# Collapsing the modulation rows with a two-column selector matmul in place of four identity transposes and a four-way sum

## The chip, the core and the metric

One core of one Trainium2 chip runs the whole program in one launch. The metric is device time in microseconds (us) of that launch. Shorter is better.

## The reference

Three blocks run one after another on 256 tokens of width 1024: a two-layer trunk with a 256-token context beside the latent sequence, a gated delta-net with its feed-forward, and a dilated attention with its feed-forward. The change touches only the modulation of the trunk, which each of its two layers computes for two conditioning vectors, `c_ctx` (the context's) and `c` (the latent's):

```python
def modulation(cvec, w_mod, b_mod):
    m = (jax.nn.silu(cvec) @ w_mod + b_mod)[..., None, :]
    return jnp.split(m, 6, axis=-1)

sh1, sc1, ga1, sh2, sc2, ga2 = modulation(c, w_mod, b_mod)
sh1c, sc1c, ga1c, sh2c, sc2c, ga2c = modulation(c_ctx[None], w_mod, b_mod)
u = (rmsnorm(x, g_mix) * (1 + sc1) + sh1) @ w_in
```

`w_mod` is 2 x 1024 x 6144, so a vector-matrix product of 1024 x 6144 is made for two vectors in each layer. Its results scale and shift the normed activations, and gate what is added to the residual.

## The kernel before, in words

**Layout.** Activations in column form have the model dimension on the 128 partitions, so a modulation value must end up as a per-partition scalar: MODC (a part of the small-tile buffer SM) holds 192 columns, [layer, sequence, which of six, block of 128 channels]. The 6144 outputs of a layer are made in 12 chunks of 512; with two layers there are 24 chunks, numbered m = 0 to 23.

**One chunk** takes four steps on three engines.

1. `pe_modulate(m)` (TensorE, PE): two weight tiles of 1 MB (RAW, from DMA), eight matmuls of 512 moving columns. The stationary operand is SC2, the two silu vectors padded with zeros to 32 columns. Four of the eight go to partition groups 0, 32, 64 and 96 of one PSUM bank at a time, so the bank holds four partial sums: partition 32 g + s holds group g's part for vector s, and the partitions with s of 2 or more hold zeros.
2. `act_modulate(m)` (ScalarE, ACT): copies the bank, 128 x 512, to ROWS, which is CF[:, 1024:1536]. There is one ROWS buffer, so the copy of chunk m waits for the turn of chunk m - 1 (`pe_mod`).
3. `pe_modturn(m)` (PE, the "turn"): four transposes of 128 x 128, with ROWS as the stationary operand and the identity IDN (CF[:, 0:128]) as the moving one. They fill a bank of 128 x 512. The last one raises `pe_mod`.
4. `dve_modturn(m)` (VectorE, DVE): a TENSOR_REDUCE that picks the columns 32 g + s (s below 2) of each of the four blocks and adds over g: 32 values in and 8 out on each partition. It raises `dve_mod`, frees the bank, and later `dve_modend` adds the bias and makes the gains.

**Order.** Each engine runs its own instruction stream, written out by hand with semaphores; `weave` interleaves generators step by step. `pe_start` does chunks 0 to 3 at the head of the kernel, before anything else can be projected: modulate(0), modulate(1), turn(0), modulate(2), turn(1), modulate(3), turn(2), turn(3), then the transposes of the small vectors ("cols") and of the normed input. Chunks 4 to 23 are woven by `mods(...)` into the projections, the mixers and the MLPs of the trunk, up to about half of the span. On the sequences of PE, ACT and DVE a turn lies between long runs of weight matmuls. Weights are split into two fp32r halves (WHI by ACT, WLO by DVE), and `matmul3` makes three matmuls of them.

**The head of the DVE stream** (`dve_start`): three memsets (the last one clears SC2), then a wait for the transposes of the silu vectors ("crow"), then the copy of these into SC2, which `pe_modulate(0)` needs. The identity arrives by a DMA that SP issues as its third (`ld_id`).

**CF[:, 1024:1920]** holds ROWS (1024:1536) and SC2 (1536:1792) in the trunk; columns 1792 and up are not used then. POOL loads the level masks over all of it once turn 23 is done.

The helper lines under which the trace records instructions: L69 `matmul`, L77 `transpose`, L80 `act`, L83 `copy`, L86 `tt`, L99 `reduce`, L108 `memset`.

Of the kernel before, what the change touches and what calls it, by code (L numbers as in the profile page):

```python
# [9 lines left out]
ALU = mybir.AluOpType  # L10
# [171 lines left out]
def program(nc, T, out):  # L182
    ctx = ExitStack()
    with ctx:
        def sb(name, n, dt=F32):
            return ctx.enter_context(nc.sbuf_tensor(name, [128, n], dt))
# [16 lines left out]
        CF = sb("CF", 2304)  # L203
# [21 lines left out]
        def cf(i, n=128):  # L225
            return CF[:, 128 * i:128 * i + n]
        IDN, TRIF, TRIB, SSUF, SPRE, ONE16, MSKT, MSKN = [cf(i) for i in range(8)]
# [5 lines left out]
        def small(n):  # L233
            a = at[0]
            at[0] += n
            assert at[0] <= 1744
            return SM[:, a:a + n]
# [4 lines left out]
        MODC = small(192).rearrange("p (l s j k) -> p l s j k", l=2, s=2, j=6)  # L242
# [21 lines left out]

        ROWS = CF[:, 1024:1536]
        SC2 = CF[:, 1536:1792].rearrange("p (k s) -> p k s", k=8)
        CROW = AR[0:2, 0:1024]

        signals = []

        def signal(name, by=1):
            s = Signal(ctx.enter_context(nc.semaphore(name)), by)
            signals.append(s)
            return s


        ld_c, ld_id, ld_x, ld_ctx, ld_small, ld_wg, ld_cf, ld_mu, ld_gf, ld_row, ld_di, ld_lm, ld_xr, st_out = [
            signal(n, 16) for n in ("ld_c", "ld_id", "ld_x", "ld_ctx", "ld_small", "ld_wg", "ld_cf", "ld_mu",
                                    "ld_gf", "ld_row", "ld_di", "ld_lm", "ld_xr", "st_out")]
        w_land = [signal(f"w_land{i}", 16) for i in range(NRAW)]  # L280

        act_c, dve_c, pe_c, pool_c = [signal(n) for n in ("act_const", "dve_const", "pe_const", "pool_const")]
# [25 lines left out]
        pe, act, dve, pool, sp = [Engine() for _ in range(5)]  # L308

        def wait_free(key):  # L310

            had = banks.before.get(key)
            if had is None or pe.eng is None:
                return
            for s in signals:
                if ("free", had) in s.at:
                    pe.wait_ge(s, ("free", had))
                    return
            raise KeyError(had)
# [161 lines left out]
        def pe_modulate(m):  # L481
# [4 lines left out]
            for k0 in (0, 4):  # L486
# [3 lines left out]
                for k in range(4):  # L490
                    i = pe.matmul(b[32 * k:32 * k + 32, :], SC2[:, k0 + k, :], v[:, k, :], k0 == 0, k0 == 4)
                i.then_inc(pe_gemm, ("used", t.i), ("mod", m))
# [7 lines left out]
        def pe_modturn(m):  # L500
            b = banks.take(("modt", m), ring)
            wait_free(("modt", m))
            pe.wait_ge(act_mod, ("row", m))
            for i in range(4):
                o = pe.transpose(b[:, 128 * i:128 * i + 128], ROWS[:, 128 * i:128 * i + 128], IDN)
            o.then_inc(pe_mod, ("turn", m))

        def dve_modturn(m):
            l, ch = chunks[m]
            dve.wait_ge(pe_mod, ("turn", m))  # L510
            b = banks.of(("modt", m))
            parted = b.rearrange("p (k g c) -> p c k g", k=4, g=4)[:, 0:2]
            dve.reduce(MODC[:, l, :, ch // 2, 4 * (ch % 2):4 * (ch % 2) + 4], parted, ALU.add).then_inc(
                dve_mod, ("free", ("modt", m)), ("col", m))

        VCv = VC[:, 0:64].rearrange("p (v l k) -> p v l k", v=4, l=2)
# [4 lines left out]
        def dve_modend(l, c0, c1):  # L521
            js = slice(c0 // 2, c1 // 2)
            dve.wait_ge(dve_mod, ("col", 12 * l + c1 - 1))
            dve.wait_ge(dve_c, "cols")
            for sq in range(2):
                dve.tt(MODC[:, l, sq, js], MODC[:, l, sq, js], BMv[:, l, js], ALU.add).then_inc(dve_mod, ("bias", l, c1))
            dve.wait_ge(dve_mod, ("bias", l, c1))
            for j in range(2):
                if c0 <= 6 * j + 2 < c1:
                    for sq in range(2):  # L530
                        dve.stt(GS[:, l, sq, j, :], MODC[:, l, sq, 3 * j + 1, :], 1.0, VCv[:, j, l, :], ALU.add, ALU.mult).then_inc(
                            dve_mod, ("gain", l, j))
# [4 lines left out]
        def pe_mods(ms):  # L537
            for m in ms:
                pe_modulate(m)
                yield  # L540
                pe_modturn(m)
                yield
# [54 lines left out]
        def dve_norm(t, ti, had=None, row=None):  # L597

            dve.wait_ge(pool_tn, ("rstd", t, ti))
            if had is not None:  # L600
                dve.wait_ge(pe_tn, ("turn", t, had, 1))
                if row is None:
                    dve.wait_ge(dve_tn, ("lo", t, had, 1))
            xb, s = XNb[ti % 2], s_tn[ti][:, 0:1]
            if row is None:
                dve.ts(xb, XRt[:, ti, :], s, None, ALU.mult).then_inc(dve_tn, ("xn", t, ti))
            else:
                dve.stt(xb, XRt[:, ti, :], s, row, ALU.mult, ALU.mult).then_inc(dve_tn, ("xn", t, ti))
# [70 lines left out]
        def small_loads():  # L679
            for i, n in enumerate(("g_mix", "g_mlp", "norm_mix_2", "norm_ffn_2")):  # L680
                yield vr[16 * i:16 * i + 16, :], T[n].rearrange("l (k p) -> (l k) p", p=128)
            yield vr[64:68, :], T["s_pool"].rearrange("l (k p) -> (l k) p", p=128)
            yield v_ap[0:96, 1, :], T["b_mod"].rearrange("l (k p) -> (l k) p", p=128)
            yield CWR, T["gdn_conv_w_2"].rearrange("a w (k p) -> (a w k) p", p=128)
            for l in range(2):
                yield GQK[:, l, 0, :], T["g_q"][l, :].partition_broadcast(128)
                yield GQK[:, l, 1, :], T["g_k"][l, :].partition_broadcast(128)
                yield GGLA[:, l, :], T["g_gla"][l, :].partition_broadcast(128)
                yield WP[:, l, :, :], T["w_pool"][l].rearrange("(a b) c d -> (b c) a d", b=2)
            yield GNW, T["gdn_norm_w_2"][0, :].partition_broadcast(128)  # L690
            yield DQK[:, 0, :], T["dil_q_norm_2"][0, :].partition_broadcast(128)
            yield DQK[:, 1, :], T["dil_k_norm_2"][0, :].partition_broadcast(128)
            yield ALD[:, 0:8], T["gdn_a_log_2"][0, :].partition_broadcast(128)
            yield ALD[:, 8:16], T["gdn_dt_bias_2"][0, :].partition_broadcast(128)

        def sp_start():
            sp.dma(CROW[0:1, :], T["c_ctx"].rearrange("(a n) -> a n", a=1)).then_inc(ld_c, "c_ctx")
            sp.dma(CROW[1:2, :], T["c"]).then_inc(ld_c, "c")
            sp.dma(CF[:, 0:128], T["cf"][:, 0:128]).then_inc(ld_id, "idn")

        def pe_start():
# [3 lines left out]
            for k in range(8):  # L705
                m = pe.transpose(b[:, 2 * k:2 * k + 2], CROW[:, 128 * k:128 * k + 128], IDN[0:2, 0:2])
            m.then_inc(pe_c, "crow")
# [15 lines left out]
        def act_start():  # L723
            act.dma(XRt[:, 2:4, :], T["x"][0].rearrange("(t p) d -> p t d", p=128)).then_inc(ld_x, "x")
            act.dma(XRt[:, 0:2, :], T["ctx"][0].rearrange("(t p) d -> p t d", p=128)).then_inc(ld_ctx, "ctx")
            act.wait_ge(ld_c, "c")
            act.act(CROW, CROW, ACT.Silu).then_inc(act_c, "silu")
            for o, i in small_loads():
# [16 lines left out]
        def dve_start():  # L745
            dve.memset(R8[0:33, 512:1536], 0.0).then_inc(dve_c, "wz")
            dve.memset(RT[32:33, :], 1.0).then_inc(dve_c, "ones")
            dve.memset(SC2, 0.0).then_inc(dve_c, "sc0")
            dve.wait_ge(pe_c, "crow")
            dve.wait_ge(dve_c, "sc0")  # L750
            dve.copy(SC2[:, :, 0:2], banks.of("crow")[:, 0:16].rearrange("p (k s) -> p k s", k=8)).then_inc(dve_c, ("free", "crow"), "sc")
            dve_norm("in0", 0)
            dve_norm("in0", 1)
            for m in range(4):
                dve_modturn(m)
            b = banks.of("cols")
            dve.wait_ge(pe_c, "cols")
            dve.copy(VC, b[:, 0:68])
            dve.copy(BMC, b[:, 128:224])
            dve.copy(CWC, b[:, 256:352]).then_inc(dve_c, ("free", "cols"), "cols")  # L760
            dve_modend(0, 0, 4)
            for ti in range(4):
                dve_turned("in0", ti, True)
                if ti < 2:
                    dve_norm("in0", ti + 2, ti)
            dve.wait_ge(ld_mu, "mu")
            dve.copy(MU[:, :], AR[:, 12544:13568]).then_inc(dve_c, "mu")
            dve_splits(proj_tile(NAMES[0], 0, 0, 0))
# [47 lines left out]
        def proj_tile(name, l, sq, c):  # L816
            return tile_of["w_in", (l, sq), 4 * c, COLS[name][0]]
# [2851 lines left out]
```

## Time and profile before

| | |
|---|---|
| median of 3 runs | 2021.7 us |
| lowest and highest run | 2015.37 and 2022.43 us |
| the profiled execution's own time | 2015.37 us |
| its span | 2013.6 us |
| TensorE clock granted, mean of the span | 0.958 of full |
| PE busy | 1839.6 us, 91% |
| DVE busy | 1230.7 us, 61% |
| ACT busy | 927.3 us, 46% |
| DMA | 320.43 MB, mean 159 GB/s |

The profiled execution is the lowest of the three runs shown. Its span leaves 1.8 us of its own time outside. In the rows below, PE is a matmul, PEld a weight load, which overlaps the matmuls. The tile names read "output <- inputs", and for a matmul the moving operand stands first and the stationary one second, then the rows x columns of the stationary tile, then the partitions x moving columns. A matmul's duration covers its whole way through the array; matmuls overlap, so what one costs in a stream is the distance from one start to the next, not its duration.

### The profile page before, as it was taken

To read this page: it belongs to the slowest core of one execution; us is meant where nothing else is said; L and a number is where in the kernel's file an instruction comes from. 1 tells how busy PE (TensorE), PEld (TensorE's weight loads), DVE (VectorE), ACT (ScalarE), POOL (GpSimd) and SP (SyncE) were. 2 spreads that over 40 slices of the span, in tenths; PEclk is the share of its full clock that TensorE was granted. 3 is DMA by queue.
4 is the path that set the end of the run, shared out by engine and by line. 5 is a ranking of instruction groups with operands and counts; after the bars stand their busy time and mean duration, and the time that the engine had idled before them with its cause. 6 is when DMAs were issued, how large, how long until landed. Compare 5 with 4: busy or idle time off the path is not lost.

```text
span 2013.6 us, 26348 instructions
## 1 busy us (share of the span) xinstructions
PE 1839.6 (91%) x10729; PEld 1512.3 (75%) x10729; DVE 1230.7 (61%) x1700; ACT 927.3 (46%) x1433; POOL 381.1 (19%) x428
## 2 busy tenths in 40 slices
PE   4879787999999999877989989898999999989999
PEld 1756566777887777765778879897878878877887
DVE  2555547566676665566465756863577646567774
ACT  3544344355456443544354547445344434454442
POOL 2121122211141122121111222121211005321110
PEclk9889998899999999898889999999999999999999
DMA  8454553355556576531355654221255554414554
GB/s 288 143 198 143 188 179 119 123 187 169 195 168 225 189 246 215 174 99 43 117 186 192 190 176 133 85 75 52 86 172 186 187 180 167 167 53 153 192 189 136
DMA packets 218244, 320.43 MB, mean 159 GB/s; under 512 B 8582, under 2 KB 123978, under 8 KB 217740
## 3 DMA queue, kind: packets, MB, share of 16 engines
q1 hardware_dynamic: 212916, 308.97, 47.3%
q0 software_dynamic: 1744, 6.03, 0.9%
q10 hardware_dynamic: 3464, 3.75, 0.6%
q8 instruction: 85, 1.39, 0.3%
q14 instruction: 35, 0.29, 0.0%
HBM read 317.68 MB, written 1.05 MB: 158 GB/s over the span
## 4 chain that ended last, share of the span: by engine, by line
PE 74%; DVE 10%; ACT 7%; DMA 5%; issue 3%; POOL 2%; SPq 0%; ACTq 0%; DVEq 0%; POOLq 0%
PE ps L69 71%; PE ps L77 3%; DVE WLO L86 3%; DMA RAW<-in_w_mod_dram 2%; ACT WHI L80 2%; DMA RAW<-in_w_up_dram 1%; DMA RAW<-in_w_in_dram 1%; ACT AR L80 1%; DVE AR L86 1%; DVE TT L86 1%; ACT PMD L80 1%; ACT L80 1%; POOL SM L86 1%; DVE PMD L86 1%; ACT TT L80 1%
## 5 line engine op out<-in xcount | busy, mean ns | idle before, releaser
L86 DVE TENSOR_TENSOR WLO<-RAW,WHI 128x1024 fp32r<-128x1024 f32 (+2 forms) x498 | 604.3, 1255 | 320.0 <-ACT WHI L80 319.6
L80 ACT ACTIVATE WHI<-RAW 128x1024 fp32r<-128x1024 f32 (+2 forms) x498 | 482.0, 1017 | 403.3 <-PE ps L69 309.1
L69 PE MATMUL ps<-TT,WHI 128*128 128x512 f32 (+1 forms) x1808 | 578.5, 380 | 10.2 <-DVE TT L86 7.1
L69 PE MATMUL ps<-TT,WLO 128*128 128x256 f32 x1632 | 429.7, 281 | 0.0
L69 PE MATMUL ps<-WHI,TT 128*128 128x512 f32 (+2 forms) x1200 | 373.5, 385 | 27.4 <-DVE WLO L86 24.1
L69 PEld LDWEIGHTS ps<-TT,WHI 128*128 128x128 f32 x1808 | 322.4, 191 | 70.0 <-issue 11.3
L69 PE MATMUL ps<-WHI,ARR 128*128 128x512 f32 x1120 | 354.8, 393 | 7.9 <-DVE ARR L86 4.3
L69 PEld LDWEIGHTS ps<-TT,WLO 128*128 128x128 f32 x1632 | 312.3, 191 | 14.6
L69 PEld LDWEIGHTS ps<-WHI,TT 128*128 128x128 f32 x1200 | 226.0, 195 | 79.0 <-DVE WLO L86 29.9
L69 PEld LDWEIGHTS ps<-WHI,ARR 128*128 128x128 f32 x1120 | 210.2, 188 | 59.3 <-issue 9.2
L69 PE MATMUL ps<-WLO,TT 128*128 128x512 f32 (+2 forms) x600 | 225.5, 376 | 0.0
L69 PE MATMUL ps<-WLO,ARR 128*128 128x512 f32 x560 | 218.2, 390 | 0.0
L86 POOL TENSOR_TENSOR AR<-AR 128x512 f32<-128x512 f32 x70 | 85.6, 1223 | 522.2 <-ACT ARR L80 292.3
L80 ACT ACTIVATE AR<-ps 128x256 f32<-128x256 f32 (+3 forms) x183 | 81.6, 467 | 142.9 <-PE ps L69 78.9
L99 DVE TENSOR_REDUCE AR<-ps 128x256 f32<-128x512 f32 x184 | 125.8, 685 | 32.7 <-PE ps L69 31.9
L69 PEld LDWEIGHTS ps<-WLO,TT 128*128 128x128 f32 x600 | 117.2, 195 | 16.5
L86 POOL TENSOR_TENSOR XR<-XR,AR 128x512 f32<-128x512 f32 (+1 forms) x50 | 72.0, 1445 | 268.3 <-DVE AR L86 249.1
L69 PEld LDWEIGHTS ps<-WLO,ARR 128*128 128x128 f32 x560 | 105.2, 188 | 20.8
L86 POOL TENSOR_TENSOR SM<-SM 128x1 f32<-128x1 f32 (+4 forms) x87 | 75.1, 864 | 121.7 <-DVE SM L93 54.0
L80 ACT ACTIVATE AR<-AR 128x512 f32<-128x512 f32 (+3 forms) x88 | 53.0, 605 | 89.8 <-DVE AR L99 85.5
L77 PE MATMUL ps<-CF,AR 128*128 128x128 f32 (+2 forms) x392 | 63.3, 286 | 33.4 <-DVE AR L86 12.1
L77 PEld LDWEIGHTS ps<-CF,AR 128*128 128x128 f32 (+2 forms) x392 | 46.8, 146 | 45.4 <-issue 24.2
(195 smaller groups left out, 1832.0 us busy)
## 6 DMA issues: line engine op xcount, KB each, us to landing
RAW<-in_w_mod_dram SPq DMA_DIRECT2D x48, 1024.0 KB, 5.6
RAW<-in_w_up_dram SPq DMA_DIRECT2D x48, 1024.0 KB, 5.6
RAW<-in_w_down_dram SPq DMA_DIRECT2D x48, 1024.0 KB, 5.1
RAW<-in_ffn_w_in_dram SPq DMA_DIRECT2D x44, 1024.0 KB, 5.1
RAW<-in_w_in_dram SPq DMA_DIRECT2D x20, 1024.0 KB, 5.6
RAW<-in_ffn_w_out_dram SPq DMA_DIRECT2D x20, 1024.0 KB, 5.1
RAW<-in_dil_w_in_dram SPq DMA_DIRECT2D x18, 1024.0 KB, 4.8
RAW<-in_gdn_w_in_dram SPq DMA_DIRECT2D x16, 1024.0 KB, 5.6
```

What stands on the lines that cost most here:

```text
L69: return Made(None if self.eng is None else self.eng.matmul(o, l, r, start=start, stop=stop))
L77: return Made(None if self.eng is None else self.eng.transpose(o, i, idn))
L80: return Made(None if self.eng is None else self.eng.activation(o, i, f, **k))
L86: return Made(None if self.eng is None else self.eng.tensor_tensor(o, a, b, op))
L99: return Made(None if self.eng is None else self.eng.tensor_reduce(o, i, AX.X, op, **k))
```

## The change

A tile SEL of 128 x 2 is made once, at the head of the DVE stream, in CF[:, 1792:1794]: DVE waits for the identity and adds up its column groups, so SEL[p, s] is 1 where p modulo 32 equals s. The turn then uses ROWS as the stationary operand as before, but an ordinary matmul with SEL's two columns moving in place of a transpose with the identity's 128. It selects and adds the four partial sums in one go, so its output for a block is 128 x 2, and the four blocks take 8 columns of the bank. DVE copies these 8 values to MODC, in place of the reduce over 32.

```diff
+        SEL = CF[:, 1792:1794]
...
             wait_free(("modt", m))
             pe.wait_ge(act_mod, ("row", m))
             for i in range(4):
-                o = pe.transpose(b[:, 128 * i:128 * i + 128], ROWS[:, 128 * i:128 * i + 128], IDN)
+                o = pe.matmul(b[:, 2 * i:2 * i + 2], ROWS[:, 128 * i:128 * i + 128], SEL, True, True)
             o.then_inc(pe_mod, ("turn", m))
...
-            parted = b.rearrange("p (k g c) -> p c k g", k=4, g=4)[:, 0:2]
-            dve.reduce(MODC[:, l, :, ch // 2, 4 * (ch % 2):4 * (ch % 2) + 4], parted, ALU.add).then_inc(
+            dve.copy(MODC[:, l, :, ch // 2, 4 * (ch % 2):4 * (ch % 2) + 4], b[:, 0:8].rearrange("p (k s) -> p s k", s=2)).then_inc(
                 dve_mod, ("free", ("modt", m)), ("col", m))
...
             dve.memset(SC2, 0.0).then_inc(dve_c, "sc0")
+            dve.wait_ge(ld_id, "idn")
+            dve.reduce(SEL, IDN.rearrange("p (g c) -> p c g", g=4)[:, 0:2, :], ALU.add).then_inc(dve_c, "sel")
             dve.wait_ge(pe_c, "crow")
             dve.wait_ge(dve_c, "sc0")
```

## Rows read from the trace of the kernel before

**Rows 1.** The page, part 1: busy time by engine.

```profile
PE 1839.6 (91%) x10729; PEld 1512.3 (75%) x10729; DVE 1230.7 (61%) x1700; ACT 927.3 (46%) x1433; POOL 381.1 (19%) x428
```

**Rows 2.** The page, part 4: the chain that ended last, by engine.

```profile
PE 74%; DVE 10%; ACT 7%; DMA 5%; issue 3%; POOL 2%; SPq 0%; ACTq 0%; DVEq 0%; POOLq 0%
```

**Rows 3.** Groups by form: busy us, mean ns | idle before, its releasers.

```profile
L77 PE MATMUL ps<-CF 128*128 128x128 f32 x96 | 15.8, 289 | 7.1 <-ACT AR L80 4.7 <-ACT CF L80 2.0 <-DVE R L83 0.4
...
L99 DVE TENSOR_REDUCE SM<-ps 128x8 f32<-128x32 f32 x24 | 4.5, 187 | 30.7 <-PE ps L77 30.7
...
L83 DVE COPY AR<-ps 128x8 f32<-128x8 f32 x4 | 0.4, 154 | 0.0
...
L80 ACT ACTIVATE CF<-ps 128x512 f32<-128x512 f32 x24 | 14.2, 592 | 50.5 <-PE ps L69 35.0 <-PE ps L77 15.5
```

**Rows 4.** Timeline around turn 13: start us, us, instruction, count.

```profile
427.57 0.39 PE L69 MATMUL ps<-WHI,ARR 128*128 128x512 f32 x1
...
427.80 0.60 PE L77 MATMUL ps<-CF 128*128 128x128 f32 x4
...
428.15 0.48 PE L69 MATMUL ps<-WHI,ARR 128*128 128x512 f32 x1
...
428.44 0.19 DVE L99 TENSOR_REDUCE SM<-ps 128x8 f32<-128x32 f32 x1 [0.53 <-PE ps L77]
```

**Rows 5.** Timeline of PE, sixteen transposes in a stream of weight matmuls.

```profile
1350.18 1.91 PE L77 MATMUL ps<-CF,AR 128*128 128x128 f32 x16
1351.85 0.48 PE L69 MATMUL ps<-WHI,TT 128*128 128x512 f32 x1
```

**Rows 6.** Timeline of PE, ordinary matmuls of 8 and of 1 moving column.

```profile
1244.44 0.96 PE L69 MATMUL ps<-AR,CF 128*128 128x8 f32 x8
1245.25 1.93 PE L69 MATMUL ps<-CF,X 128*128 128x1 f32 x16
1247.04 0.48 PE L69 MATMUL ps<-TT,WHI 128*128 128x256 f32 x2
```

**Rows 7.** Timeline of PE: one moving column after idle time; 128 columns in a stream.

```profile
1254.10 1.05 PE L69 MATMUL ps<-CF,X 128*128 128x1 f32 x8 [0.27 <-ACT X L80]
...
1262.33 3.73 PE L69 MATMUL ps<-CF,SM 128*128 128x128 f32 x32
```

**Rows 8.** Timeline of the first 10 us: the head of the kernel.

```profile
2.67 0.27 DVE L108 MEMSET CF<- 128x256 f32 x1
...
8.66 0.98 PE L77 MATMUL ps<-CF,AR 2*128 2x2 f32 x8 [8.66 <-DMA CF<-in_cf_dram]
...
9.68 0.17 DVE L83 COPY CF<-ps 128x16 f32<-128x16 f32 x1 [6.74 <-PE ps L77]
...
13.27 1.94 PE L69 MATMUL ps<-RAW,CF 128*32 128x512 f32 x8 [3.62 <-DMA RAW<-in_w_mod_dram]
```

**Rows 9.** Timeline from 27 to 43 us: turns 0, 2 and 3.

```profile
27.93 1.12 PE L77 MATMUL ps<-CF 128*128 128x128 f32 x4
...
29.87 1.94 PE L69 MATMUL ps<-RAW,CF 128*32 128x512 f32 x8 [0.81 <-DMA RAW<-in_w_mod_dram]
...
37.78 1.06 PE L69 MATMUL ps<-RAW,CF 128*32 128x512 f32 x8 [0.41 <-DMA RAW<-in_w_mod_dram]
38.78 0.66 PE L77 MATMUL ps<-CF 128*128 128x128 f32 x4
...
39.53 0.60 ACT L80 ACTIVATE CF<-ps 128x512 f32<-128x512 f32 x1 [3.33 <-PE ps L77]
...
40.27 0.78 PE L77 MATMUL ps<-CF 128*128 128x128 f32 x6 [0.84 <-ACT CF L80]
...
41.17 0.56 DVE L83 COPY SM<-ps 128x68 f32<-128x68 f32 x3
```

**Rows 10.** Busy time by stretch; the column behind POOL is the granted clock.

```profile
1008.00:1024.00 16.00, 7.82 (x36) 6.35 (x35) 11.49 (x22) 9.84 (x20) 2.80 (x6) 0.68 0.70 237
1024.00:1100.00 76.00, 76.00 (x402) 65.12 (x401) 49.01 (x53) 34.35 (x42) 11.87 (x10) 1.00 0.57 180
```

## The prediction

> **What bounds the kernel now.** I read the page's busy times first. PE is busy for 91% of the span, DVE for 61%, ACT for 46% [rows 1]. The chain that ended last says the same: 74% of it is PE, 10% DVE, 7% ACT [rows 2]. So a change pays in full only where it takes time out of PE's stream, or shortens a wait that PE stands in. I then asked for the groups by form, to see how large the changed work is. The 96 transposes of the 24 turns are 15.8 us of busy PE, under 1% of its 1839.6 us, and PE stood idle for 7.1 us before them, waiting for ACT's data mostly. The 24 reduces are 4.5 us, 187 ns each, of DVE's 1230.7 us [rows 1, 3]. Busy time overstates PE's part, since matmuls overlap. What a turn costs PE shows in a timeline: the next weight matmul starts 0.35 us after the first transpose (427.80 to 428.15) [rows 4], so 24 turns take about 24 x 0.35 = 8.4 us of PE's stream at full clock, 0.4% of the span. That is the most that a turn costing nothing could return there.
>
> **The change, part by part.**
>
> *PE, the four matmuls.* The number of instructions stays: four weight loads of 128 x 128 from ROWS and four matmuls. Only the moving operand shrinks, from 128 columns to 2. The question is whether columns or the weight load set the distance between starts. For the transposes I take 16 in a row: 1.91 us less the last one's 0.27, over 15, is 0.109 us [rows 5]. No matmul with two columns is in the trace, but there are some with 8 and with 1. Sixteen with one column have (1.93 - 0.25) / 15 = 0.112 us, where 0.25 is the duration of one (1.05 us for eight less seven times 0.112 gives 0.27) [rows 6, 7]. So a matmul with one column follows the last no sooner than a transpose with 128: the columns are hidden behind the loading of the stationary tile, which the change leaves alone. Two columns lie between 1 and 8, and the eight matmuls with 8 columns need no more (0.81 us to the next start, against 8 x 0.112 = 0.90). I take 0.112.
>
> For a whole turn the edges count too. 24 narrow matmuls, from the first start to the next weight matmul, took 1247.04 - 1244.44 = 2.60 us; less 20 x 0.112 that leaves 0.36 us for four, against 0.35 for a turn now [rows 4, 6]. That is +0.01 us, and the two roundings allow up to +0.02. Over 24 turns it makes +0.2 to +0.5 us if every turn lies on the path; I take +0.3. The same roundings (0.01 us on each side of a turn) set the lower end of this term at -0.2.
>
> *PE, the time to the result.* The last matmul's result comes sooner, since it has two columns to stream. After idle time, four transposes take 0.66 us to the last end (38.78) [rows 9]; eight narrow ones took 1.05, so four are 1.05 - 4 x 0.112 = 0.60 [rows 7], 0.06 us less. In a stream, 0.96 for eight less 0.45 is 0.51, against 0.60, 0.09 us less [rows 4, 6]. Who waits for that? ACT's copy of the next chunk and DVE's reduce. Of ACT's 50.5 us of waits before these copies 35.0 are for the matmuls of the chunk and 15.5 for the transposes, and those 15.5 are in the head [rows 3]. Turns 0 and 1 stand before a weight DMA: PE is idle after them until data land (0.81 us of it at 29.87) [rows 9], so they return nothing. Turn 2 is on the path: modulate(3) ends, turn 2 runs from 38.78 for 0.66, ACT's copy starts at 39.53, turn 3 at 40.27 [rows 9]. That is one gain of 0.06 us. Behind turn 3, DVE's copies of the small vectors (41.17) wait for transposes that PE issues after the turn, so it counts as PE stream only. In the rest of the trunk the consumer of MODC comes many matmuls later.
>
> *DVE, the read.* A reduce of 32 to 8 values takes 187 ns; a copy of 8 values from PSUM 154 ns [rows 3]. That is -33 ns, 24 times, -0.8 us of DVE. DVE holds a tenth of the chain [rows 2], so I count a tenth, -0.1 us; the ends are 0 and -0.8.
>
> *DVE, the new wait and reduce at the head.* The wait for the identity stands behind three memsets; queued behind it on DVE are only the copy of the silu vectors and later work. DVE is idle for 6.74 us before that copy, and the copy waits for eight small transposes, which themselves waited for the identity until 8.66 and took 0.98 us. So the reduce of 8 values, at most 0.19 us by the larger reduce, runs from about 8.7 to 8.9 and the copy still starts at 9.68. The work that hides it is those transposes. With that cover gone it would cost 0.19 us, and even that falls into PE's wait for w_mod, 3.62 us before 13.27 [rows 3, 8]. I take 0, with 0.2 as the upper end. No DMA is added or moved; POOL's load over CF still waits for turn 23, so SEL stays whole.
>
> *The sum.* +0.3 - 0.1 - 0.1 + 0 = +0.1 us on the profiled execution's 2015.37 us, thus 2015.5. The ends: -0.2 - 24 x 0.09 - 0.8 = -3.2 us, if each turn's latency and each DVE saving came off the path; +0.5 + 0.2 = +0.7 us. The profiled run is the fastest of three and lies 6.3 us below their median. A median of the changed kernel should be read against the median: 2021.7 + 0.1 = 2021.8 us. The three runs differ by 7 us, 0.35%, so 0.5% (10 us) is about what can be told from no change here, and both ends of my sum are well inside.
>
> **A rule against the change.** Ordinary fp32 matmuls with 128 moving columns on a 128 x 128 stationary tile stand (3.73 - 0.27) / 31 = 0.112 us apart, only 3 ns more than transposes [rows 5, 7]. The Trainium skill, TensorE: Matmul & The Clock Gate, Terms, says that the weight load and the matmul have a transpose mode which is four times faster for fp32. By that rule, read as a price for every load and matmul that leaves the mode, the sum would be some 31 us higher, an estimate from the page; by the row it is +0.3 us, so the trace doesn't agree with it for this pair of operations. What such a price would do here is worked out from rows as the second rival.
>
> **The rivals.**
>
> 1. *The turn's latency is on the path nearly everywhere.* Then -3.2 us, 2018.5. For it: ROWS is a single buffer, and ACT waits for the turn. Against: outside the head ACT's waits name the chunk's matmuls [rows 3].
> 2. *Slower: for this operand the ordinary weight load and matmul take four times what a transpose takes.* 96 x 3 x 0.109 = +31 us, 2053. Point of decision: the start-to-start distance in a turn; from 0.22 us up (96 x 0.11 = 10.6 us) it decides. For it: nothing in the rows, only that a two-column form with ROWS has not run. Against: rows 6, with 128 x 128 loads at 0.112.
> 3. *The clock falls more often.* At 1008 to 1024 us, where PE was busy for 7.8 of 16 us, the granted clock was 0.68; in the dense stretch behind it 1.00 [rows 10]. In the head, matmuls took 1.94 us for eight at 29.87 and 1.06 at 37.78 [rows 9], so 1.2 GHz before and 2.4 GHz after. A turn with 2 columns in place of 128 gives the array less to do, and one more stretch of some 10 us at half the clock costs up to 5 us in dense work. Two would be needed for 10 us, 2032. Against: next to each turn lie matmuls of 512 columns by the hundred.
> 4. *The clock rises sooner or falls less.* If the narrow matmuls count for more than the transposes, the head returns at most the 0.88 us of one modulate, and one 10 us stretch less later 5 us, two 10 us: 2011. The Trainium skill, the same page, Part 4: PE-mode transpose, says that transposes don't count as PE being busy in the same way; no row here separates them from the idle time about them.
> 5. *The identity comes late and DVE holds up the head.* Then PE's transposes are late as well; 2021.9.
>
> **How the numbers follow.** The forecast (nothing beyond 1 us, with rival 5) has 0.80, rival 1 0.08, rival 2 0.02, rival 3 0.05, rival 4 0.05. Rival 1 falls within 0.5%. So faster has 0.05, same 0.88, slower 0.07. The range takes in the ends of the sum and one stretch of clock either way on top of the runs' spread: low is the lowest run less the 3.2 us of rival 1, 2012; high is the highest run, plus 0.7 and one 5 us stretch, 2028. Outside are rivals 2, 3 and most of 4.
>
> **What would show it in the profile after.** The turns stand as L69 matmuls of 128x2, 96 of them, 0.11 us apart, and the next weight matmul starts 0.35 to 0.37 us after the first; 0.2 us or more apart would be rival 2, and a distance well below 0.1 would mean that the columns did set it, a gain of some us. The turn's end after idle at about 38.8 us comes 0.60 us after its start, and ACT's copy moves up by 0.06. DVE shows 24 copies of about 154 ns, one new reduce near 8.7 us and the silu copy still near 9.7. PE's busy sum falls by 1 to 2 us, as each duration is shorter, without the span following. The mean granted clock stays within 0.01 of 0.958; a fall of 0.005 or more, in stretches beside turns, would be rival 3.

## The result and the profile after

The changed kernel takes 2038.29 us (median of 6 runs, 2035.04 to 2043.7) against 2020.61 us before (6 runs, 2015.37 to 2022.43). The ratio is 1.009, with a 95% interval of 1.0075 to 1.0106: it is 0.9% slower, and 10 us above the top of the range that was given. Measured twice more beside other kernels, the ratio was 1.0073 (1.0055 to 1.0091) and 1.0088 (1.0074 to 1.0102). One run of the kernel before, beside the last four kernels of the table below, took 10023 us for a reason that its record does not show, and the ratios leave it out.

The page of the profiled execution (2035.04 us), part 1, answers [rows 1]:

```profile
PE 1862.9 (92%) x10825; PEld 1533.9 (75%) x10825; DVE 1230.9 (60%) x1701; ACT 927.5 (46%) x1433; POOL 380.1 (19%) x428
```

The count of PE's records is what to stop at. It rose from 10729 to 10825, by 96, though the diff replaces 96 matmuls by 96 matmuls and adds none. PE's busy time rose by 23.3 us, where a fall of 1 to 2 us was expected. DVE has one instruction more, the selector's reduce.

The groups by form of the changed kernel answer [rows 3]:

```profile
L69 PE MATMUL ps<-CF 128*128 128x2 f32 x192 | 26.7, 261 | 7.3 <-ACT AR L80 5.0 <-ACT CF L80 1.9 <-DVE R L83 0.4
...
L80 ACT ACTIVATE CF<-ps 128x512 f32<-128x512 f32 x24 | 14.2, 592 | 56.2 <-PE ps L69 56.1
...
L83 DVE COPY SM<-ps 128x8 f32<-128x8 f32 x24 | 3.9, 164 | 38.8 <-PE ps L69 38.7
```

Each ordinary fp32 matmul stands as two records, each with its own weight load: 192 for the 96 of the 24 turns. Each is a little shorter (261 against 289 ns), and there are twice as many. Around turn 13, the timeline of PE answers [rows 4]:

```profile
441.28 0.39 PE L69 MATMUL ps<-WHI,ARR 128*128 128x512 f32 x1
441.51 0.95 PE L69 MATMUL ps<-CF 128*128 128x2 f32 x8
442.31 0.49 PE L69 MATMUL ps<-WHI,ARR 128*128 128x512 f32 x1
```

From the first matmul of the turn to the next weight matmul it is now 442.31 - 441.51 = 0.80 us, against 0.35 before. In this document a pass is one such record, a weight load with its matmul. The passes are (0.95 - 0.25) / 7 = 0.10 us apart on average; the first step is short (0.03 us) and the other six are 0.112 each. The distance that I read for a matmul is that of a pass, and an ordinary fp32 matmul has two. With the edges a turn costs +0.45 us of PE's stream, 24 turns 24 x 0.45 = 10.8 us.

The head, in the timeline of the first 48 us, answers [rows 8, 9]:

```profile
8.56 0.17 DVE L99 TENSOR_REDUCE CF<-CF 128x2 f32<-128x8 f32 x1 [5.61 <-DMA CF<-in_cf_dram]
...
8.68 0.98 PE L77 MATMUL ps<-CF,AR 2*128 2x2 f32 x8 [8.68 <-DMA CF<-in_cf_dram]
...
9.69 0.18 DVE L83 COPY CF<-ps 128x16 f32<-128x16 f32 x1 [0.96 <-PE ps L77]
...
34.73 1.87 PE L69 MATMUL ps<-CF 128*128 128x2 f32 x8
...
40.25 1.20 PE L69 MATMUL ps<-CF 128*128 128x2 f32 x8
...
41.55 0.60 ACT L80 ACTIVATE CF<-ps 128x512 f32<-128x512 f32 x1 [4.26 <-PE ps L69]
...
42.29 1.02 PE L69 MATMUL ps<-CF 128*128 128x2 f32 x8 [0.84 <-ACT CF L80]
```

The selector costs nothing: it is made from 8.56 to 8.73, and the silu copy starts at 9.69, as before. Turn 1 takes 1.87 us, where turns 0 and 1 took 1.12 each before (27.93 and 34.39). Turn 3, the same work, takes 1.02 us at 42.29, so at 34.73 PE ran at the lower of its two levels, 1.2 GHz. The profile's clock column does not show this: it reads 1.00 for the first 37 us of the kernel before, while eight records of 512 columns took 1.94 us there (29.87) and 1.06 at 37.78. In the first stretch of the tables below it is not to be relied on.

Busy time by stretch, first of the kernel before, then of the changed one. The bounds are the starts of the same ACT instructions in both; the number behind POOL is the granted clock, as a share of 2.4 GHz.

```profile
0.00:48.20 48.20, 22.27 (x115) 7.67 (x115) 9.97 (x29) 15.09 (x34) 10.11 (x28) 0.99 0.88 301
48.20:190.30 142.10, 119.95 (x703) 92.47 (x703) 75.71 (x120) 68.43 (x121) 23.15 (x42) 0.92 0.45 153
190.30:307.50 117.20, 92.73 (x610) 67.29 (x609) 64.81 (x109) 46.19 (x83) 25.32 (x31) 0.91 0.57 184
307.50:1017.50 710.00, 653.08 (x3765) 518.73 (x3764) 447.48 (x604) 328.17 (x509) 151.18 (x159) 0.95 0.52 165
1017.50:2013.60 996.10, 951.59 (x5543) 826.15 (x5541) 632.73 (x840) 469.41 (x688) 171.29 (x170) 0.97 0.45 146
```

```profile
0.00:50.70 50.70, 26.49 (x129) 12.36 (x130) 10.09 (x30) 15.11 (x34) 11.13 (x33) 0.93 0.86 287
50.70:197.90 147.20, 125.83 (x714) 97.09 (x713) 76.00 (x120) 68.50 (x122) 21.89 (x37) 0.88 0.44 148
197.90:318.60 120.70, 97.83 (x634) 71.92 (x633) 64.94 (x109) 46.21 (x84) 25.43 (x31) 0.89 0.55 179
318.60:1040.50 721.90, 663.11 (x3814) 528.11 (x3813) 447.55 (x604) 328.27 (x509) 150.56 (x159) 0.94 0.51 163
1040.50:2034.60 994.10, 949.67 (x5542) 824.39 (x5541) 632.34 (x840) 469.39 (x688) 171.06 (x170) 0.98 0.45 146
```

The stretches grew by 2.5, 5.1, 3.5, 11.9 and -2.0 us. Everything lost is lost in the head and the trunk, where the turns are. But the second stretch holds only three turns (1.4 us at 0.45) and grew by 5.1, with the clock at 0.88 in place of 0.92; the fourth holds twelve (5.4 us) and grew by 11.9, with 0.94 in place of 0.95. So the two traces suggest two parts: some 11 us of added passes, and more time at half clock in the trunk. The mean clock of the span is 0.952 against 0.958. At half clock that makes 2 x 0.048 x 2034.6 = 195 us against 2 x 0.042 x 2013.6 = 169. These are single executions, 21.0 us apart where the medians are 17.7 apart, and the one of the kernel before is its fastest; the runs below ask how much belongs to the change.

### The profile page after: what moved, and what is told of

The parts are those of the page before. It is cut to its first block, busy times and chain, and to the rows that moved or that the text cites. A ratio compares the mean times of both kernels' runs of the same rounds, so it can differ in the third digit from the quotient of the medians.

```text
span 2034.6 us, 26541 instructions
## 1 busy us (share of the span) xinstructions
PE 1862.9 (92%) x10825; PEld 1533.9 (75%) x10825; DVE 1230.9 (60%) x1701; ACT 927.5 (46%) x1433; POOL 380.1 (19%) x428
## 4 chain that ended last, share of the span: by engine, by line
PE 74%; DVE 9%; ACT 7%; DMA 5%; issue 3%; POOL 2%; SPq 0%; ACTq 0%; DVEq 0%; POOLq 0%
PE ps L69 72%; PE ps L77 3%; DVE WLO L86 3%; DMA RAW<-in_w_up_dram 2%; ACT WHI L80 1%; DMA RAW<-in_w_in_dram 1%; DMA RAW<-in_w_mod_dram 1%; DVE AR L86 1%; ACT AR L80 1%; ACT PMD L80 1%; DVE TT L86 1%; POOL SM L86 1%; DVE PMD L86 1%; ACT L80 1%; ACT TT L80 1%
## 5 line engine op out<-in xcount | busy, mean ns | idle before, releaser
L69 PE MATMUL ps<-TT,WHI 128*128 128x512 f32 (+1 forms) x1808 | 580.7, 381 | 12.2 <-DVE TT L86 7.0
L69 PE MATMUL ps<-WHI,TT 128*128 128x512 f32 (+2 forms) x1200 | 372.9, 384 | 27.1 <-DVE WLO L86 23.3
L69 PEld LDWEIGHTS ps<-TT,WHI 128*128 128x128 f32 x1808 | 323.6, 192 | 72.3 <-issue 12.2
L69 PEld LDWEIGHTS ps<-TT,WLO 128*128 128x128 f32 x1632 | 313.2, 192 | 14.7
L69 PEld LDWEIGHTS ps<-WLO,ARR 128*128 128x128 f32 x560 | 105.2, 188 | 20.9
```

Of the source, the lines that this page charges most:

```text
L69: return Made(None if self.eng is None else self.eng.matmul(o, l, r, start=start, stop=stop))
```

## The experiments

All ratios are to the kernel before in runs on the same chip, with 95% intervals. "Passes" are matmul records of a turn; the kernel before has four and the changed kernel eight. "The last block" is the last feed-forward, behind the trunk. The texts set off before each result were written before its runs.

| run | what differs from the kernel before | us | before beside it | ratio |
|---|---|---|---|---|
| e1_twice | transposes twice, 8 passes | 2033.69 | 2021.5 | 1.0063 (1.0047 to 1.0079) |
| e2_wide | ordinary, 128 columns, 8 passes | 2035.34 | 2021.5 | 1.0069 (1.0051 to 1.0087) |
| e3_onepass | narrow, fp32r, 4 passes | 2020.02 | 2021.5 | 0.9997 (0.9986 to 1.0009) |
| e4_late | 96 transposes in the last block | 2031.68 | 2021.5 | 1.0055 (1.0038 to 1.0072) |
| a_again | the change, 8 passes | 2035.68 | 2021.02 | 1.0073 (1.0055 to 1.0091) |
| e2_again | as e2_wide | 2037.4 | 2021.02 | 1.0081 (1.0063 to 1.01) |
| e5_head | the change for chunks 0 to 3 | 2020.25 | 2021.02 | 1.0006 (0.9992 to 1.002) |
| e6_rest | the change for chunks 4 to 23 | 2034.53 | 2021.02 | 1.0065 (1.0046 to 1.0085) |
| a_third | the change | 2038.14 | 2019.02 | 1.0088 (1.0074 to 1.0102) |
| e7_five | transposes five times, 20 passes | 2048.13 | 2019.02 | 1.0137 (1.0121 to 1.0154) |
| e8_late4 | 384 transposes in the last block | 2061.15 | 2019.02 | 1.0201 (1.0186 to 1.0216) |
| e9_mixed | two ordinary wide ones before each transpose, 20 passes | 2053.67 | 2019.02 | 1.0167 (1.0145 to 1.0189) |
| e7_again | as e7_five | 2046.91 | 2020.36 | 1.0152 (1.0126 to 1.0177) |
| e9_again | as e9_mixed | 2051.41 | 2020.36 | 1.0157 (1.013 to 1.0184) |
| e10_narrow | as e9_mixed with two columns, 20 passes | 2060.7 | 2020.36 | 1.0193 (1.0166 to 1.022) |
| e1_again | as e1_twice | 2032.98 | 2020.36 | 1.0061 (1.0045 to 1.0078) |

**Is it the number of passes?** Three kernels change only what a turn issues.

```diff
 # e1_twice, against the kernel before
             for i in range(4):
+                pe.transpose(b[:, 128 * i:128 * i + 128], ROWS[:, 128 * i:128 * i + 128], IDN)
                 o = pe.transpose(b[:, 128 * i:128 * i + 128], ROWS[:, 128 * i:128 * i + 128], IDN)
 # e2_wide, against the kernel before; the reduce stays
-                o = pe.transpose(b[:, 128 * i:128 * i + 128], ROWS[:, 128 * i:128 * i + 128], IDN)
+                o = pe.matmul(b[:, 128 * i:128 * i + 128], ROWS[:, 128 * i:128 * i + 128], IDN, True, True)
 # e3_onepass, against the changed kernel
+        CFr = alias("CFR", 2304, F32R, cf0)
+        ROWSr, SELr = CFr[:, 1024:1536], CFr[:, 1792:1794]
-                o = pe.matmul(b[:, 2 * i:2 * i + 2], ROWS[:, 128 * i:128 * i + 128], SEL, True, True)
+                o = pe.matmul(b[:, 2 * i:2 * i + 2], ROWSr[:, 128 * i:128 * i + 128], SELr, True, True)
```

In the last one ACT writes ROWS as fp32r, and DVE copies the selector to fp32r.

> The kernel before with each of a turn's four transposes issued twice: eight single-pass 128-column instructions per turn, no selector, the old reduce. Theory A (an ordinary fp32 matmul goes through the array twice, so the changed turn has eight passes of 0.11 us in place of four, and everything lost comes from that): as slow as the changed kernel, 2035 to 2041 us against 2020.6, ratio 1.007 to 1.011. Rival B (two moving columns leave the array less active, and part of the loss is clock that falls for it): only the passes' own price, 24 x 0.44 = 10.5 us, so about 2031, and fewer microseconds at half clock than in the changed kernel. Rival C (the loss is in the head, from the selector or the new wait): no change, 2020.6.

> The kernel before with the four transposes replaced by ordinary fp32 matmuls with the same 128-column identity, and the old reduce; no selector. Theory A: the columns don't matter, so 2035 to 2041 us as in the changed kernel, with 192 matmul records for the 24 turns, 0.11 us apart. Rival B: the array is kept as busy as by transposes for twice as long, so the clock falls less than in the changed kernel, about 2031 us. Rival C: 2020.6.

> The changed kernel with ROWS and the selector held as fp32r, so that a turn's matmuls are single-pass; it drops the low bits of the modulation values that fp32r doesn't hold. Theory A: the loss is gone, 2018 to 2023 us, 96 matmul records, the next weight matmul 0.36 us after the first of a turn. Rival B: the array is even less active (four passes of two columns), so the clock falls as often as in the changed kernel, and at least 7 us of the loss stays: 2027 us or more. Rival C: the selector and its wait are still there, 2038.

The groups by form of these three, in order:

```profile
L77 PE MATMUL ps<-CF 128*128 128x128 f32 x192 | 26.2, 281 | 6.9 <-ACT AR L80 4.5 <-ACT CF L80 2.1 <-DVE R L83 0.4
```

```profile
L69 PE MATMUL ps<-CF 128*128 128x128 f32 x192 | 29.5, 302 | 5.8 <-ACT AR L80 4.6 <-ACT CF L80 0.8 <-DVE R L83 0.4
```

```profile
L69 PE MATMUL ps<-CFR 128*128 128x2 f32 x96 | 15.1, 261 | 8.2 <-ACT AR L80 4.4 <-ACT CFR L80 3.4 <-DVE R L83 0.4
```

The one-pass kernel keeps the selector, the two columns, the copy in place of the reduce and the wait at the head, and drops only the second pass; the loss is gone (-0.03%). Its rival B, that two columns alone let the clock fall, had asked for 2027 us or more, so it is out for single-pass turns. Its turn in a stream of weight matmuls, in the timeline of PE:

```profile
433.58 0.50 PE L69 MATMUL ps<-CFR 128*128 128x2 f32 x4
433.94 0.49 PE L69 MATMUL ps<-WHI,ARR 128*128 128x512 f32 x1
```

0.36 us to the next weight matmul: just what I had forecast for the change, for a matmul that is one pass. Doubled transposes, with neither selector nor narrow operand, lose 12.2 us, between the band of theory A and the 10.5 us of rival B; the wide matmuls lose 13.8 us, at the lower end of theory A's band. So the passes are the cause of most of the loss, and rival C (head, selector, wait) is out.

**What does a pass cost where PE is never short of work?**

```diff
 # e4_late (e8_late4 has range(16), and i % 4 for the place in the bank)
                 need(k)
+                if k == 0 and key[:2] == ("f", 1) and key[2] < 6:
+                    for i in range(4):
+                        pe.transpose(b[:, 128 * i:128 * i + 128], IDN, IDN)
```

> The kernel before with 96 transposes of the identity (four at the head of each of 24 accumulation groups) added to the last feed-forward block, where PE is busy all the time at full clock; the trunk is untouched. Theory A with a fixed price: 96 x 0.109 = 10.5 us, so 2031, all of it as PE stream. If the 18 us of the changed kernel are more than the passes' own price because they fall into the trunk with its waits and clock falls, this run shows the difference: 10.5 here against 18 there. If a pass cost more than its distance (a fixed cost for switching between kinds of matmul), this run would show 18 us too.

96 passes gave +10.2 us, for 10.5 by the price: going into transposes and back 24 times adds no fixed cost that can be measured. At this price some 11 us of the change's loss are its stream. The remaining 4 to 8 us of the three measurements (+17.7, +14.7, +19.1) stand above that price.

**Where in the trunk?** The changed kernel and the wide one again, and the change split by chunk (`if m < 4` and `if m >= 4`; the other chunks keep transposes and reduce).

> The changed kernel once more, beside the other three of this set. It measured +17.7 us against the kernel before, while doubled transposes gave +12 and the 128-column ordinary matmuls +14. If that difference is chance or chip, this run comes out at +12 to +15 us; if two-column matmuls cost more than 128-column ones (theory A, fallen in its size: latency, clock, or the head), it stays at +17 to +19.

> The 128-column ordinary matmuls with the old reduce once more, for the comparison with the changed kernel on one chip. Theory A (only passes count): within 3 us of the changed kernel. Rival B (narrow columns let the clock fall): 4 us or more below it.

> Narrow ordinary turns for chunks 0 to 3 alone, transposes and reduces for the other twenty. Theory A with the head's own state: three of the four turns run at half clock there (1.87 us in place of 1.12), and the last two lie on the path, so +1.5 to +3 us. If the head carried the surplus of the changed kernel over the passes' price, this would be +6 us or more. No effect of the head: below +1.

> Narrow ordinary turns for chunks 4 to 23, transposes for the four of the head. Theory A: 20 x 0.46 = 9.2 us of PE stream at full clock, up to 12 with the stretches at half clock. With additive shares it and the run of the head alone add up to the changed kernel's own loss; if that is 17 to 18 us, this run should show 14 to 16.

The head alone changes nothing that can be measured (-0.8 us by the medians, -0.1% to +0.2%), although its turns take longer; I had expected +1.5 to +3. The other twenty turns lose 13.5 us, just under the 14 to 16 that I wrote down, for 20 x 0.45 = 9.0 us of stream. On this chip the change lost 14.7 and the wide matmuls 16.4, in the other order than before, so at this dose narrow and wide can't be told apart by their times.

**Does the surplus over the price scale?** Four times the dose, in the turn and in the last block.

```diff
 # e7_five
             for i in range(4):
+                for _ in range(4):
+                    pe.transpose(b[:, 128 * i:128 * i + 128], ROWS[:, 128 * i:128 * i + 128], IDN)
                 o = pe.transpose(b[:, 128 * i:128 * i + 128], ROWS[:, 128 * i:128 * i + 128], IDN)
 # e9_mixed; e10_narrow has b[:, 128 * i:128 * i + 2] and IDN[:, 0:2]
+                for _ in range(2):
+                    pe.matmul(b[:, 128 * i:128 * i + 128], ROWS[:, 128 * i:128 * i + 128], IDN, True, True)
                 o = pe.transpose(b[:, 128 * i:128 * i + 128], ROWS[:, 128 * i:128 * i + 128], IDN)
```

> The kernel before with each transpose of a turn issued five times: 16 extra passes a turn, 384 in all, in the place of the turn. So far four extra passes a turn gave +12 to +18 us in the trunk, while 96 extra passes in the last feed-forward gave +10.2. Theory A with the price alone: 384 x 0.109 = 41.9 us, about 2063. Theory D (a pass in the trunk costs 1.3 to 1.5 times its distance, through half clock and waits around it): 54 to 63 us, about 2075 to 2084. Theory E (a fixed surplus of some 4 us from the changed phase of the trunk, whatever the dose): 46 us, 2067.

> The kernel before with 384 transposes of the identity in the last feed-forward (16 at the head of 24 accumulation groups). All theories: the price alone, 41.9 us, about 2063; it is the yardstick for the five-fold turns.

> The kernel before with two ordinary 128-column fp32 matmuls put ahead of each of a turn's transposes, to the same place in the bank, so again 16 extra passes a turn, but by ordinary matmuls. Theory A: 384 x 0.112 = 43 us, 2064; within 3 us of the five-fold transposes in any case where only the count of passes matters. If ordinary passes cost more than transposing ones in this place (a switch of mode), it lies 5 us or more above the five-fold transposes.

> The changed kernel a third time, beside the dose runs on one chip. +17.7 and +14.7 us before; theory A with the price alone 11 us, theory D 14 to 16, theory E 15.

The yardstick held: 384 passes in the last block cost 42.1 us, 0.110 each. All three theories on the turn fell. Five-fold transposes cost only 29.1 us there, less than their own price, not more. The changed kernel, a third time, lost 19.1 us, more than any of the three gave it. The stretches of the five-fold run, bounded by the same ACT instructions, show where the difference arises:

```profile
53.30:199.30 146.00, 124.88 (x753) 96.79 (x752) 75.63 (x120) 68.36 (x121) 19.27 (x28) 0.92 0.45 149
199.30:319.70 120.40, 100.02 (x689) 75.16 (x688) 65.18 (x109) 46.25 (x83) 25.25 (x31) 0.95 0.55 179
319.70:1050.80 731.10, 675.99 (x3958) 541.46 (x3957) 446.77 (x604) 328.41 (x509) 151.69 (x159) 0.95 0.50 161
```

From 199.3 to 319.7 us PE is busy for 7.3 us more than in the kernel before in that stretch, and the stretch is only 3.2 us longer. Part of the added stream fills time in which PE waited (24.5 us without a matmul before, 20.4 here), and the clock is 0.95 where it was 0.91. In this stretch the changed kernel had 0.89. The stretch holds five turns, 5 x 16 x 0.109 = 8.7 us of added stream. The next one, where PE waits less, holds twelve, 20.9 us, and is 21.1 us longer. So the price holds in dense work and shrinks where PE waits. The part behind the last turn, 4.7 us shorter than before, holds no added pass. In these profiles passes in the trunk act in three ways: they push work back by their own length, they fill waits, and the time at half clock changes with them, in either direction.

**Narrow or wide, ordinary or transposing?**

> As the mixed run (16 extra passes a turn by two ordinary fp32 matmuls ahead of each transpose), but with two moving columns in place of 128. If only the count of passes matters: within 3 us of the mixed run on this chip, about +33 us. If narrow passes let the clock fall (rival B at four times the dose): 8 us or more above it, with a lower granted clock.

> The mixed run once more (128 columns). Count of passes alone: equal to the five-fold transposes within 3 us; ordinary passes dearer than transposing ones: 5 us or more above them again, as the first time (+35 against +29).

> The five-fold transposes once more. +29 us the first time, against 41.9 us of added stream; if part of that stream again fills time in which PE waited or would have fallen to half clock, +27 to +31 here.

> The doubled transposes once more. +12 us the first time. If the surplus of the changed kernel (+14.7 to +19 for the same number of passes) comes with ordinary matmuls, this stays at +11 to +13; if it is a matter of chip and chance, +14 to +17.

Narrow against wide: +40 us against +31, 9.3 us by the medians, although a turn's stream is no longer (in the timeline of the narrow run it is 1.96 us to the next weight matmul, in that of the wide one 2.13):

```profile
446.08 0.50 PE L69 MATMUL ps<-CF 128*128 128x2 f32 x4
...
448.04 0.48 PE L69 MATMUL ps<-WHI,ARR 128*128 128x512 f32 x1
```

```profile
441.88 0.60 PE L69 MATMUL ps<-CF 128*128 128x128 f32 x4
...
444.01 0.48 PE L69 MATMUL ps<-WHI,ARR 128*128 128x512 f32 x1
```

The stretch that holds turns 7 to 11, in the narrow and then in the wide run:

```profile
200.50:324.00 123.50, 103.06 (x691) 77.65 (x690) 65.72 (x109) 46.33 (x83) 25.53 (x31) 0.91 0.54 175
```

```profile
198.70:319.50 120.80, 100.87 (x689) 75.86 (x688) 65.10 (x109) 46.29 (x83) 25.16 (x31) 0.95 0.55 179
```

The clock is 0.91 with narrow passes and 0.95 with wide ones. So the dearer run went with the lower clock in this stretch, as rival B has it; but the intervals (1.0166 to 1.022 and 1.013 to 1.0184) still meet. It is likely and not settled. Ordinary against transposing: +31.1 against +26.6 by the medians here, +34.7 against +29.1 before; both times about 5 us, with intervals that overlap both times. Doubled transposes repeat at +12.6, in the band that I had written down for a surplus that comes with ordinary matmuls.

**The granted clocks of all runs.** The profiles are single executions, but the record has the mean granted clock of every run. Time at half clock is worked out from it, as 2 x (1 - clock) x span; the clocks have three decimals, and 0.001 is 4 us of it. The surplus is the loss less the added stream. That is, by the distances to the next weight matmul, 24 x 0.44 us for the doubled transposes, 24 x 0.45 for the change (4 x and 20 x for its parts), 24 x 0.46 for the wide kernel, 24 x 0.01 for the one-pass one, and 24 x 1.78 and 24 x 1.61 for sixteen wide and narrow passes; for added transposes alone it is their number x 0.109.

| kernel | runs | clock, median (range) | us at half clock | surplus, us |
|---|---|---|---|---|
| before, in four sets | 53 | 0.955 to 0.956 (0.952 to 0.958) | 178 to 182 | |
| one-pass narrow turn | 12 | 0.956 (0.954 to 0.959) | 178 | -1.7 |
| the change in the head alone | 12 | 0.956 (0.953 to 0.959) | 178 | -2.6 |
| doubled transposes, twice | 12 | 0.9545 (0.953 to 0.957) | 185, 185 | +1.6, +2.1 |
| wide ordinary, twice | 12 | 0.9535 (0.952 to 0.956) | 189, 191 | +2.8, +5.3 |
| the change, in its three measurements | 17 | 0.951 (0.950 to 0.953) | 199.5, 199.3, 199.5 | +6.9, +3.9, +8.3 |
| the change for chunks 4 to 23 | 6 | 0.951 (0.950 to 0.954) | 199 | +4.5 |
| sixteen transposes more, twice | 9 | 0.960 (0.956 to 0.963) | 162, 164 | -12.8, -15.4 |
| sixteen wide passes more, twice | 10 | 0.9575 (0.954 to 0.962) | 172, 177 | -8.1, -11.7 |
| sixteen narrow passes more | 5 | 0.953 (0.949 to 0.959) | 193 | +1.7 |
| 96 and 384 transposes in the last block | 10 | 0.957 (0.952 to 0.959) | 174, 173 | -0.3, +0.2 |

Four narrow ordinary matmuls in a turn go with 18 to 22 us more at half clock than before, wide ones with 8 to 10, doubled transposes with 3. The last line leaves the trunk as it was and has 4 to 7 us less than before, so a difference of that size is within chance. A microsecond at half clock costs at most half a microsecond, so 18 to 22 us cost up to 9 to 11, an estimate that covers the surplus of 4 to 8 us. The order of the surpluses is the order of the clocks in nearly every line. On one chip, beside each other, the six runs of the change have 0.950 to 0.953 and the six of the wide kernel 0.952 to 0.955. So narrow and wide do differ in the clock, even where their times can't be told apart, and the one-pass turn shows that two columns alone, in half as many passes, do not lower it. Why the clock answers so is not shown.

## Why the prediction was wrong, step by step

**What bounds the kernel: right.** PE's stream did set the price: a pass put into the last block or into the dense part of the trunk is paid for. The four turns of the head are not paid for in any measurable way.

**The cost of a matmul in the turn: this is the step that failed.** The prediction said that "the distance between starts" of an ordinary matmul was 0.112 us, from "sixteen with one column" in [rows 6], and hence +0.01 us a turn. The sixteen records are eight matmuls of two passes. (The duration of the last one stands there as 0.25 and as 0.27 us; both give 0.11.) Likewise the 24 records behind the edges of a turn are twelve matmuls, and the eight behind the time to the result are four. Read so, the same rows give 2.60 - 16 x 0.112 = 0.81 us for a turn, and 0.80 was measured. The distance between passes was right, 0.112; per matmul it is 0.224, against 0.109 for a transpose, and a turn costs +0.45 us and not +0.01. The trace of before had the sign in a row that I quoted: in [rows 8], eight RAW,CF records stand for one weight tile, for which `pe_modulate` issues four matmuls, while the eight transposes of the silu vectors are eight records. Counting the records of one operation against the loop that issues it would have given 24 x 0.45 = 10.8 us, and the other side of the 0.5%.

The rule weighed there was the one of the Trainium skill, TensorE: Matmul & The Clock Gate, Terms, that transpose mode is four times faster for fp32. Measured, a transpose is 2.05 times as fast as an ordinary fp32 matmul with a stationary tile of the same size (0.109 against 0.224 us), not four times, and not just as fast, as I took it to be. Another page of the Trainium skill, FP8 and Floating Point Precision, TensorE Precision Notes, says that a true fp32 matmul takes four passes through the array; I had not used it. The records show two for each, at a distance of 0.112 us.

**The same step in the rival.** Rival 2 named this mechanism, with a threshold: "from 0.22 us up (96 x 0.11 = 10.6 us) it decides". The measured distance is 0.224. It got a chance of 0.02, because the rows were read as matmuls. With the price at two and not four times, its 31 us would have been 11.

**The columns: right.** They don't set the distance: 128-column ordinary matmuls, in the wide runs, cost as much as the change within the spread. That it is the weight load that sets the distance was argued, and no run here changes the load alone. The time to the result fell per pass (261 against 289 ns), but rose per turn. The gain of 0.06 us on ACT's copy in the head thus turned into a delay: from the start of turn 2 to that copy it was 0.75 us before (38.78 to 39.53) and is 1.30 us now (40.25 to 41.55). PE was also not idle right after turn 1, as the prediction has it (its next matmuls start at 35.44, with no wait); its next wait, of 0.41 us, is the one at 37.78.

**DVE: right.** The copies take 164 ns (154 forecast, 187 before). The selector's reduce took 0.17 us from 8.56, and the silu copy moved from 9.68 to 9.69. The one-pass run, which has all of this, is at 0.9997: the saving on DVE is worth nothing that can be measured.

**The clock: underrated.** Rival 3 had one stretch of half clock in mind as chance, and a fall of 0.005 in the mean as its sign. Over all runs the fall is 0.004 to 0.005, from 0.955 or 0.956 to 0.951. The measurements exceed the price of the passes by 4 to 8 us, and the added time at half clock, 18 to 22 us, is enough for that. The reason given, two columns in place of 128, holds only in part: the one-pass turn has two columns and keeps 0.956. The clock and the surplus go together; that the one causes the other is argued, not shown. Rival 4 took transposes to count for less than ordinary matmuls, but with sixteen more of them in a turn the clock rose, to 0.960. What stays open is why narrow ordinary passes go with a lower clock, and how much of the surplus each part of the trunk gives. That 384 passes cost 42 us in the last block and 27 to 29 us in the turns shows that the trunk does not add up linearly.

No run beats the kernel before; the best, the one-pass turn, equals it and holds the modulation in fp32r.

## What to carry to other kernels

Before a distance between records is taken as the cost of an operation, count the records of one such operation against the loop in the code that issues it. Replacing a transpose by an ordinary fp32 matmul doubled the weight loads and the matmul records here, and with a 128 x 128 stationary tile the cost doubled with them, with 2 moving columns as with 128. In a part that waits now and then, an added pass cost neither nothing nor its length; measure there, and keep a yardstick of the same dose in a dense part beside it. Before a change of clock is read from one profile, look at the granted clock of every run: the kernel before alone has 0.952 to 0.958.

## What the runs showed of the hardware that was not expected

- An ordinary fp32 matmul is recorded as two weight loads and two matmuls, 0.112 us apart, with 2 or 128 moving columns; a transpose of fp32 data as one of each, 0.109 us; an fp32r matmul with two columns as one of each (96 records for 96 matmuls), four of them taking 0.36 us to the next matmul.
- 384 transposes cost 42.1 us in the last block, where PE is nearly always busy, and 29.1 and 26.6 us in the turns of the trunk.
- With 16 extra passes a turn, two-column ones ran 9.3 us longer in all than 128-column ones, with 0.91 against 0.95 as the granted clock of one stretch, though their stream was 0.17 us shorter per turn.
- At four extra passes a turn the time at half clock was 199 us with narrow ordinary passes, 189 and 191 with wide ones and 185 with transposes, against 178 to 182 before.
